# Four layer norms with the variance taken from raw squares: mean square less squared mean

## What is computed

```python
def layer_norm(x, g, b):
    mu = jnp.mean(x, axis=-1, keepdims=True)
    var = jnp.mean(jnp.square(x - mu), axis=-1, keepdims=True)
    y = (x - mu) * lax.rsqrt(var + LN_EPS)
    return y * g + b

for layer in range(2):
    mix = recurrent_mixer(h, ...) if layer == 0 else fox_mixer(h, ...)
    h = layer_norm(DN_ALPHA * h + mix, ln1_g[layer], ln1_b[layer])
    h = layer_norm(DN_ALPHA * h + conv_ffn(h, ...), ln2_g[layer], ln2_b[layer])
```

## Time and profile before

| what | value |
| --- | --- |
| median of three timed runs | 3219.47 us (3218.55 to 3222.94) |
| the profiled execution's own time | 3215.47 us |
| its span, first to last instruction | 3213.7 us |
| PE busy | 3146.8 us, 98% of the span |
| DVE, ACT, POOL busy | 2016.9, 1027.7, 1730.2 us |
| the four norms, first mean copy | at 284.70, 690.42, 1079.78 and 1477.39 us |

### The profile page before, as it was taken

One profiled execution on the slowest core, in us unless ns is written; L12 is line 12 of the kernel. 1 busy time (PEld: TensorE's weight loads), 2 busy tenths in 40 slices (PEclk: granted clock), 3 DMA queues, 4 the chain that ended last, 5 costly groups with the idle time before them and its releaser, 6 DMA issues.

```text
span 3213.7 us, 50071 instructions
## 1 busy us (share of the span) xinstructions
PE 3146.8 (98%) x16578; PEld 2526.7 (79%) x16578; DVE 2016.9 (63%) x4168; ACT 1027.7 (32%) x2258; POOL 1730.2 (54%) x1555
## 2 busy tenths in 40 slices
PE   8999999999999999999999999999999999999998
PEld 7787888877777788886446888878888688788887
DVE  6686767765555666876446554466677634376776
ACT  3543333023333333302326343123330334223320
POOL 4343887762221488783001433458878532478877
PEclk9999999999999999999999999999999999999999
DMA  3223223211111222221110111222232111222231
GB/s 133 87 86 125 79 86 105 88 57 60 53 53 40 99 86 99 105 79 53 66 46 29 64 59 59 79 79 86 99 112 73 61 65 66 79 75 90 99 105 53
DMA packets 68771, 250.63 MB, mean 78 GB/s; under 512 B 7568, under 2 KB 7568, under 8 KB 68544
## 3 DMA queue, kind: packets, MB, share of 16 engines
q1 hardware_dynamic: 68544, 247.72, 22.3%
HBM read 245.59 MB, written 2.10 MB: 77 GB/s over the span
## 4 chain that ended last, share of the span: by engine, by line
PE 87%; DVE 4%; POOL 3%; ACT 3%; issue 2%; DMA 0%; DVEq 0%; SPq 0%; POOLq 0%; ACTq 0%
PE psum L2709 36%; PE psum L2756 15%; PE psum L806 6%; PE psum L2646 5%; PE psum L2945 4%; PE psum L2237 3%; POOL scratch L3866 3%; PE psum L1770 3%; PE psum L1797 2%; PE psum L2262 1%; PE psum L838 1%; PE psum L2957 1%; PE psum L1824 1%; PE psum L876 1%; ACT scratch L1484 1%
## 5 line engine op out<-in xcount | busy, mean ns | idle before, releaser
L3866 POOL TENSOR_TENSOR scratch<-scratch 128x512 f32<-128x512 f32 (+1 forms) x616 | 681.3, 1116 | 168.3 <-DVE scratch L3519 57.8
L2709 PE MATMUL psum<-scratch 128*128 128x256 f32 (+2 forms) x3168 | 765.7, 382 | 0.7 <-DVE stream L3641 0.5
L2709 PEld LDWEIGHTS psum<-scratch 128*128 128x128 f32 x3168 | 598.7, 190 | 97.0 <-DVE stream L3641 6.6
L3568 DVE TENSOR_TENSOR scratch<-scratch,psum 128x256 f32<-128x256 f32 (+2 forms) x720 | 298.4, 422 | 192.9 <-PE psum L2709 174.3
L3536 DVE SCALAR_TENSOR_TENSOR psum<-scratch,params,psum 128x256 f32<-128x256 f32 (+2 forms) x704 | 312.3, 485 | 50.4 <-ACT psum L3133 50.4
L3153 ACT ACTIVATE scratch<-psum 128x256 f32<-128x256 f32 (+2 forms) x320 | 123.0, 386 | 381.0 <-PE psum L2709 376.9
L3866 POOL TENSOR_TENSOR scratch<-w_ring,scratch 128x512 f32<-128x512 f32 (+1 forms) x196 | 223.3, 1145 | 11.0
L3641 DVE TENSOR_TENSOR stream<-stream,psum 128x256 f32<-128x256 f32 (+1 forms) x416 | 167.0, 418 | 91.7 <-PE psum L2709 88.6
L3866 POOL TENSOR_TENSOR scratch<-w_ring 128x512 f32<-128x512 f32 x168 | 194.4, 1157 | 51.3 <-PE psum L2709 47.1
L2709 PE MATMUL psum<-acts,scratch 128*128 128x256 f32 (+2 forms) x832 | 216.5, 382 | 1.8 <-POOL scratch L3866 1.4
L2756 PE MATMUL psum<-scratch 128*128 128x256 f32 (+2 forms) x960 | 216.4, 381 | 0.5 <-ACT scratch L3174 0.4
(11 more groups left out here) (552 smaller groups left out, 6069.5 us busy)
## 6 DMA issues: line engine op xcount, KB each, us to landing
w_ring<-units SPq DMA_DIRECT2D x335, 512.0 KB, 3.6
scratch<-units SPq DMA_DIRECT2D x128, 512.0 KB, 4.2
residual<-x_t SPq DMA_DIRECT2D x4, 528.0 KB, 6.4
out_t<-residual SPq DMA_DIRECT2D x2, 512.0 KB, 3.4
out_t<-residual SPq DMA_DIRECT2D x1, 768.0 KB, 4.3
params<-cols SPq DMA_DIRECT2D x1, 568.5 KB, 10.5
out_t<-residual SPq DMA_DIRECT2D x1, 256.0 KB, 3.3
gate_w_sb<-gate_w SPq DMA_DIRECT2D x1, 96.0 KB, 10.1
```

The source lines that it names most:

```text
L2709: mm = nc.tensor.matmul(PS[:, bank, 0:H], weights(q), moving(q), start=(opens and q == 0), stop=(q == 1), skip_group_check=True)
L3568: v.tensor_tensor(row, row, PS[:, rank_bank(j, at), 0:H], ALU.add if sign > 0 else ALU.subtract).then_inc(r_later, 1)
L3866: g.tensor_tensor(blocks([RANK_BUFFERS + o for o, _, _ in sums]), blocks([a for _, a, _ in sums]), blocks([e for _, _, e in sums]), ALU.ad ...
```

## The change

The four layer norms take the variance as the mean of the raw squares less the square of the mean. ACT squares the tiles of Z as they become whole, into scratch (`squares`), with the load of the root's table between the fourth and the fifth. POOL adds up tiles 0 to 3 into `NORM_MU` and their squares into `NORM_R` (`ln_pool`), and PE takes one matmul group for each of these sums and for each of the four other tiles and squares. ACT copies the mean and squares it, DVE subtracts the squared mean from the mean square, ACT takes the root. DVE then copies the spread mean to scratch, takes the reciprocal, and goes through the tiles in turn: subtract, multiply. The gain and the bias are both applied by ACT. `LN_FAR` is empty, so POOL subtracts nothing; it waits for the copied mean all the same.

```diff
+        LN_SUMMED, LN_FAR = KD // 2, ()
+        LN_ORDER = {True: (0, 1, 2, 3, 6, 5, 4, 7), False: (0, 1, 2, 3, 5, 7, 4, 6)}
...
-            return q_added, add_done(0, last - 1 + k // 4, "12", (k // 2) % 2)
+            return q_added, add_done(0, last - 1 + k // 4, "22" if k % 2 else "12", (k // 2) % 2)
...
+                    pe.wait_ge(*z_summed(name))
+                    summed_up(mean_squares(name, T), NORM_MU[:, 0:T], True, False)
+                    mean_of(order[4])
+                    mean_of(order[5])
+                    pe.wait_ge(*squares_summed(name))
+                    summed_up(square_sums(name, T), NORM_R[:, 0:T], True, False)
+                    square_of(order[4])
+                    mean_of(order[6])
+                    square_of(order[5])
+                    mean_of(order[7]).then_inc(shared("mean", name), 1)
+                    square_of(order[6])
+                    square_of(order[7]).then_inc(shared("var", name), 1)
...
+                if name in RESIDUAL:
+                    norm_of = {"lru_out": "lru", "fox_out": "fox"}.get(name, name)
+                    for n_th, k in enumerate(ln_order(norm_of)):
+                        if n_th == KD // 2:
+                            root_table(norm_of)
+                        act.wait_ge(*z_ready(norm_of, k))
+                        nc.scalar.activation(scratch(SQ_AT, KD, T)[:, k, :], Z[:, k, 0:T], ACT.Square).then_inc(shared("sq", norm_of), 1)
...
+                    nc.scalar.activation(squared_means(T), mean_squares(name, T), ACT.Square).then_inc(mean_squared(name)[0], 1)
+                    act.wait_ge(*variance(name))
+                    nc.scalar.activation(roots(T), roots(T), ACT.Sqrt, bias=SMALL[:, eps:eps + 1]).then_inc(shared("std", name), 1)
+                    for k in range(KD):
+                        act.wait_ge(*when(name, "sc", k + 1))
+                        nc.scalar.activation(x_of(name, k, 0, T), Z[:, k, 0:T], ACT.Identity, bias=ln_col(name, "b", k),
+                                             scale=ln_col(name, "g", k)).then_inc(shared("x", name), 1)
...
+                v.tensor_tensor(roots(T), square_sums(name, T), squared_means(T), ALU.subtract).then_inc(variance(name)[0], 1)
+                v.tensor_copy(by_quarter(LN_MEAN[:, 0:T]), spread_means(name, T)).then_inc(mean_kept(name)[0], 1)
+                v.reciprocal(roots(T), roots(T)).then_inc(shared("rec", name), 1)
+                centred(0, by_quarter(LN_MEAN[:, 0:T]))
                 for k in range(KD):
+                    if 0 < k < near:
+                        centred(k, spread_means(name, T))
+                    if k < near:
+                        dve.wait_ge(*centred_by(name, k))
+                    v.tensor_tensor(by_quarter(Z[:, k, 0:T]), by_quarter(Z[:, k, 0:T]), spread_roots(name, T), ALU.mult).then_inc(shared("sc", name), 1)
...
-                    pool.wait_ge(*when(*{"ffn0": ("lru", "ctr", KD), "ffn1": ("fox", "ctr", KD), "ffn2": ("mix", "x", KD), "ffn3": ("gla", "x", KD)}[name]))
+                    pool.wait_ge(*when(*{"ffn0": ("lru", "ctr", 2 + KD - len(LN_FAR)), "ffn1": ("fox", "ctr", 2 + KD - len(LN_FAR)), "ffn2": ("mix", "x", KD), "ffn3": ("gla", "x", KD)}[name]))
...
+                for k in range(1, LN_SUMMED):
+                    pool.wait_ge(*z_ready(name, k))
+                    g.tensor_tensor(NORM_MU[:, 0:T], Z[:, 0, 0:T] if k == 1 else NORM_MU[:, 0:T], Z[:, k, 0:T], ALU.add).then_inc(z_summed(name)[0], 1)
+                for k in range(1, LN_SUMMED):
+                    pool.wait_ge(*ln_squared(name, k))
+                    g.tensor_tensor(NORM_R[:, 0:T], squared(0) if k == 1 else NORM_R[:, 0:T], squared(k), ALU.add).then_inc(squares_summed(name)[0], 1)
+                pool.wait_ge(*mean_kept(name))
```

## The result

The changed kernel takes 3229.7 us (median of 7 runs, 3228.6 to 3237.3), where the kernel before takes 3219.5 (7 runs). The ratio is 1.004, its 95% interval 1.0028 to 1.0052. So it is slower by 0.28 to 0.52%; 3231.5 had been forecast. The profiled execution took 3228.6 us, with a span of 3226.8, 13.1 more than before; 12 had been forecast. The medians differ by 10.3 us.

What follows compares the result with a forecast made beforehand. PE is at work 3146.8 of 3213.7 us, so its waits decide. 6.9 + 5.4 - 0.7 - 0.9 = +10.7, with the clock +12: 3227.5 us profiled, plus 4.0 for the median, 3231.5; range 3223 to 3241.

Steps and rivals of the forecast that it cites:

- The head: Each norm up to its reciprocal gets shorter: by 4.1 us in lru, 5.9 in ffn0, 5.8 in fox, 5.0 in ffn1.
- The tail: After each norm's reciprocal: sixteen DVE operations, 1.355 us a pair, 10.9 us in all, 4.8 more (4.5 with 512 columns).
- The ends of the norms: DVE's end of each norm moves: lru +0.65 us, ffn0 -1.1 (-0.7 with side effects), fox -1.1, ffn1 -0.9.
- The release and the turns: Start of ffn0 and ffn1: POOL's weight sums start late and alternate with DVE; PE waits, +5.7 and +4.3 us.
- DVE's chain: Start of ffn0 and ffn1: held operations delay DVE's fourteenth further sum, +6.9 us in ffn0, +5.4 in ffn1.
- The clock: PE's granted clock falls: +0.35 us behind each of two standstills, +0.7 behind ffn0.
- Rival 1: Start of ffn0 and ffn1: POOL and DVE don't alternate, PE waits only for the sixth sum; +0.3, 3219.8 us; chance 0.13.
- Rival 2: PE's clock falls at all four norms and stays low longer: about +8 us on top, 3239.5; chance 0.09.
- Rivals 3 and 4: Third: POOL not in the way, PE runs ahead, 3211 us, 0.03. Fourth: norm heads gain 2 less each, 3239.5, 0.05.

Runs made afterwards that it cites:

- The kernel before with a late release: Kernel before, own norm, but POOL's first weight sum of ffn0 and ffn1 waits for the seventh multiplication: 3227.6 us against 3214.3, ratio 1.0035.
- the early release: Changed kernel, but POOL's first weight sum of ffn0 and ffn1 waits for the norm's first subtraction, not the last: 3214.1 us against 3214.3, ratio 0.9995.
- Filling the standstills: Changed kernel with nine further matmuls of 256 columns, results unread, in each of PE's two standstills (ffn0, ffn1): 3226.8 us, ratio 1.003.
- the two kernels with 16 groups in lru: The early release with PE alone adding lru's tiles and squares: 3215.3 us; also subtracting one tile ahead, POOL not waiting for the copied mean: 3209.9.
- the one with all three edits: The early release plus subtraction one tile ahead, PE adding squares of lru's first four tiles, one matmul between X tiles in ffn0, ffn1: 3209.9 us, ratio 0.998.

## Why the prediction was right

The forecast was 3231.5 and the measured median 3229.7. The span grew by 13.1 where 12 had been forecast, 1.1 more. The prediction then added 4.0 us, by which the median before lay over its profiled execution; here it lay 1.1 over it, 2.9 less. Together that is the 1.8. Point by point, by its own steps:

- **The head.** Reciprocal of lru forecast at 289.1, measured 288.81. In ffn0 a gain of 5.9; measured 6.0 (4.58 us from PE's first mean to its end, in place of 10.60). In ffn1 it was 5.9, not 5.0; the reciprocal ended 4.37 us after the last addition had begun, in place of 10.25. DVE's copy of the mean took 0.71 (0.69 taken, from the nearest row).
- **The tail.** 1.355 a pair forecast, 1.35 measured. The last multiplication of lru was forecast at 300.0, and it was 299.63. The additions of 264 elements had been the right row to take the price of a chained operation from. The Trainium skill (VectorE: DVE Perf Modes, section "The DRAIN you can't avoid") says of eight copies in a row that a semaphore costs nothing extra; here a pair whose multiplication waits for the subtraction just before it takes 1.35 us, and 1.23 when another stands between. For this chain the measurement decides: 0.12 us for each such wait.
- **The ends of the norms.** Behind ffn0 -0.7 was forecast and -0.8 measured (from +8.3 to +7.5), behind fox -1.1 and -1.0, behind ffn1 -0.9 and -1.0. The last of them doesn't follow from the prediction's own terms: a head 5.0 shorter and a tail 4.5 longer give -0.5, and -0.9 was written. In the trace the head gained 0.9 more than the text said, and the tail grew by 4.8 us, not by 4.5, since POOL's preparation for the mixer held the first subtraction (0.89 us, not 0.63).
- **The release and the turns, the step that decided.** POOL's start forecast at 299.3, measured 299.03, by the last subtraction. The sixth sum forecast at 310.9, measured 310.95. About 2.2 us had been forecast for each of the eight sums: the first wasn't held, four took 2.1 to 2.3, the last three 1.5 to 1.7. PE's standstill forecast from 305.5 to 311.0, measured from 305.8 to 311.0. The kernel before with a late release showed it without the new norm.
- **DVE's chain.** +6.9 forecast in ffn0, +5.96 measured (POOL's rank sums at 321.46, before 315.50); +5.4 in ffn1, +4.9 measured, on top of the +9.6 with which it was reached. The term was 0.5 to 0.9 too large: the turns delayed DVE by 6.8 us in each network (21.45 less 14.69, 21.17 less 14.40), not by 7.3, and in ffn0 moving 1 began at 300.01, not at 300.4. The 14.55 us that the prediction gives for the unheld chain is a slip; its own rows give 15.78 - 1.1 = 14.68, from which its 6.9 follows, and the early release measured 14.69.
- **The clock, the term that was mis-sized.** The prediction took +0.35 for each standstill, because PE was to have 1 us in hand against POOL (by its own figures 1.45 less 1 is 0.45). It hadn't: with the chain shorter and the low clock longer (some 5 us of work at 0.50, where the row at 1015 had shown 2.9), PE became the one that was late, by 2.3 us beyond POOL's delay in ffn0 (8.3 less 6.0) and 1.9 in ffn1 (16.3, by the product at 1131.92 before and 1148.25 after, less 14.5). Filling the standstills gave back 2.3 and 1.8 us. So 4.2 stands where 0.7 was taken. By the Trainium skill (TensorE: Matmul & The Clock Gate, section "Why this matters for your kernels"), which warns of idle gaps between bursts of matmuls, the clock falls at both standstills; the traces agree.
- **What wasn't in the sum.** The clock fell in more stages than the prediction counted. From ffn0's last DVE operation to the last addition of fox the change went from +7.5 to +9.6, where 0.7 had been taken (0.9 of it right behind the norm): 1.4 too little. In ffn1's rounds came another +1.4, and behind the mark -3.6, by two falls of the clock in the kernel before. Add the errors up: chains -1.5, the clock at the two standstills +3.5, the norms -0.2, these three +1.4 + 1.4 - 3.6. That makes +1.0, by which 13.1 differs from 12.1. That the sum came so close is in part luck.

Rival 1 (no turns, 3219.8) fell with the first trace. Rival 2 (the clock at all four norms, 3239.5) had half of its mechanism right: in the changed kernel the clock was low behind both standstills, in fox's stage and in the mixer's, but each time that cost some 1 to 2.3 us, and the second half was faster. Rivals 3 and 4 had no part: PE's (6,0) waited for moving 2, and the heads were as short as forecast.

## What to carry to other kernels

A wait that names "the last operation of a loop" keeps its meaning only as long as the loop stays where it was. When work moves behind another step, look at every wait on its counter: this change lost 10 to 17 us by one number, in a queue (POOL) that wasn't meant to be touched, and with another number the same arithmetic costs nothing that the time shows. And where operations depend on each other in pairs, put one that is independent between them: with it this version came out 0.2% under the kernel before, without it no gain could be told. Last, before an edit is credited with what a trace shows, look at the granted clock of that stretch, and at a second execution of the kernel without the edit.

## What the runs showed of the hardware

- Two engines that take turns pay for every single operation: 1.0 us of delay for each held sum of 512 elements (beside VectorE's operations of 1056 and 528 elements, both inputs in SBUF), the same for three as for seven. The Trainium skill's GPSIMD Engine Reference (section "Key points") names the contention; the price is from these traces.
- A VectorE operation that waits for the one just before it starts 0.73 us after it at 528 elements, and 0.62 where it doesn't wait; on a chain of sixteen with eight such waits that made 0.9 us.
- PE can stand in a dense run of short matmuls without any wait: 1.68 and 1.44 us behind the same instruction in the two kernels with 16 groups in lru, never with 10 or 13. The transfers were at 406 GB/s at that moment, with the DMA share at 1.01. But they were as busy in kernels that had no stand (408 GB/s from 285 to 288 us in the changed kernel, 414 in the one with all three edits), so they alone don't make it. The cause stays open.
- The clock falls move by themselves. The same 8930 PE instructions behind the mark took from 1704.5 to 1712.6 us in the profiled executions of these kernels, and the head of lru 10.5 or 12.1 us in two executions of one kernel. A gain of 1 or 2 us can be shown here in one stretch of a trace, with its clock looked at, but not on the time.
